# Eight buffers for the index rows of the samples, half of them filled twelve steps early by the other lane

## The reference, cut to what matters

```python
k_idx_all = jnp.concatenate([cache_a_kidx[page_table].reshape(db, past, IDX_D), k_idx], axis=1)
s = jnp.einsum('bqhd,bsd->bqsh', q_idx, k_idx_all)
score = jnp.einsum('bqsh,bqh->bqs', jax.nn.relu(s), w_idx) * (IDX_D ** -0.5 * IDX_H ** -0.5)
top_v, top_i = lax.top_k(score, k_top)
```

```python
a = jax.nn.gelu(jnp.einsum('nhkd,nd->nhk', W['u_tab'][e], xb))
return jnp.einsum('nhk,nhkd->nd', (g * a).astype(xb.dtype), W['v_tab'][e])
```

## Time and profile before

| what | value |
|---|---|
| runs, us | 2521.28, 2516.00, 2503.99; median 2516.0 |
| profiled execution, us | 2509.73 |
| its span, first to last instruction, us | 2508.0 |
| mean granted TensorE clock | 0.816 |
| index stage in the trace | POOL's first fetch at 1395.95 us, SP's store of the scores at 1499.41 us |

### The profile page before, as it was taken

The page is one execution under the profiler, slowest core; times in us unless marked ns, Lnnn a source line. Parts: engine busy times, 40 slices in busy tenths (PEclk is TensorE's granted clock), DMA queues, the critical chain, the costliest instruction groups (busy, mean ns, idle before and its releaser), DMA issues.

```text
span 2508.0 us, 25145 instructions
## 1 busy us (share of the span) xinstructions
PE 1859.6 (74%) x6697; PEld 1011.6 (40%) x6697; DVE 1735.6 (69%) x3914; ACT 700.6 (28%) x2084; POOL 850.7 (34%) x830
## 2 busy tenths in 40 slices
PE   7999889989799978974876686577774362965355
PEld 3458476654333333422322573344441232651021
DVE  3443567441448988589999779987558885786775
ACT  2000156640133443233332222223222121221222
POOL 1000023220023333244555443236226775332442
PEclk9899988999999989987989557788886565557657
DMA  4213150017169999588989889989999999989987
GB/s 132 59 63 104 30 194 1 1 80 323 68 268 382 382 399 376 233 366 342 417 342 420 318 334 388 385 331 400 354 357 381 345 383 418 356 336 425 380 333 313
DMA packets 171529, 722.39 MB, mean 288 GB/s; under 512 B 39706, under 2 KB 83123, under 8 KB 99387
## 3 DMA queue, kind: packets, MB, share of 16 engines
q0 software_dynamic: 84384, 577.16, 57.7%
q1 hardware_dynamic: 85426, 139.95, 15.5%
q10 hardware_dynamic: 1576, 3.66, 0.4%
HBM read 713.16 MB, written 11.61 MB: 289 GB/s over the span
## 4 chain that ended last, share of the span: by engine, by line
PE 20%; DVE 18%; DMA 14%; issue 11%; SPq 5%; POOL 3%; ACT 1%; DVEq 0%; another core or an unknown queue 0%; POOLq 0%; ACTq 0%
DVE heads_t L3762 5%; PE ex_y_ps L3824 4%; DMA ex_pairs<-in_uv_tab,e_idx 3%; DMA heads_t<-in_uv_tab,e_idx 3%; SPq L1345 3%; PE fq_mg_g_ps L2994 2%; SPq L1344 2%; PE sl_at_l_ps L2010 2%; DMA cmp_v<-in_uv_tab,e_idx 1%; DVE branch_rows_t L3767 1%; DMA branch_rows_t<-in_uv_tab,e_idx 1%; DVE heads_t L3767 1%; DVE ex_pairs L3767 1%; PE fq_mg_u_ps L3001 1%; DMA is_ch<-in_cache_a_kidx,chunk_rows 1%
## 5 line engine op out<-in xcount | busy, mean ns | idle before, releaser
L3790 ACT ACTIVATE ex_coef<-ex_dots 128x1 f32<-128x1 f32 x512 | 103.8, 203 | 1040.2 <-DVE ex_dots L3767 960.0
L3733 POOL DMA_INDIRECT ex_pairs<-in_uv_tab,e_idx x147 | 178.2, 1212 | 453.0 <-DVE heads_t L3762 177.2
L3733 POOL DMA_INDIRECT branch_rows_t<-in_uv_tab,e_idx x159 | 197.3, 1241 | 266.9 <-DVE heads_t L3762 179.9
L3733 POOL DMA_INDIRECT heads_t<-in_uv_tab,e_idx x146 | 171.7, 1176 | 252.5 <-DVE heads_t L3762 138.4
L3767 DVE CUSTOM_DVE_ANT_0 ex_pairs<-ex_pairs,heads_t 128x1024 f32<-128x1024 f32 x147 | 179.3, 1221 | 95.0 <-DMA ex_pairs<-in_uv_tab,e_idx 93.9
L3767 DVE CUSTOM_DVE_ANT_0 branch_rows_t<-branch_rows_t,heads_t 128x1024 f32<-128x1024 f32 x159 | 194.0, 1222 | 59.0 <-DMA branch_rows_t<-in_uv_tab,e_idx 54.2
L3767 DVE CUSTOM_DVE_ANT_0 heads_t<-heads_t 128x1024 f32<-128x1024 f32 x146 | 178.1, 1221 | 73.3 <-DMA heads_t<-in_uv_tab,e_idx 70.8
L848 PE MATMUL in_acc<-in_w,xn_t 128*128 128x512 f32 (+7 forms) x560 | 211.5, 534 | 6.1 <-POOLq L196 4.4
L3824 PE MATMUL ex_y_ps<-ex_pairs,heads_t 128*128 128x512 f32 x212 | 118.1, 689 | 75.1 <-ACT heads_t L3797 67.2
L3824 PE MATMUL ex_y_ps<-branch_rows_t,heads_t 128*128 128x512 f32 x224 | 125.3, 693 | 57.4 <-ACT heads_t L3797 50.7
L3792 ACT ACTIVATE ex_coef<-ex_coef,e_gate 128x1 f32<-128x1 f32 x512 | 150.8, 295 | 16.6
(11 more groups left out here) (772 smaller groups left out, 3517.5 us busy)
## 6 DMA issues: line engine op xcount, KB each, us to landing
cs_ch<-in_cache_cmp_kv SPq DMA_DIRECT2D x256, 128.0 KB
fq_wg<-in_w_gate SPq DMA_DIRECT2D x9, 2048.0 KB, 11.9
fq_wb<-in_w_branch SPq DMA_DIRECT2D x9, 1024.0 KB, 16.8
in_w<-in_w_in SPq DMA_DIRECT2D x4, 2048.0 KB, 11.6
fs_blocks<-in_w_branch SPq DMA_DIRECT2D x6, 1024.0 KB, 19.9
heads_t<-in_w_mem_kv SPq DMA_DIRECT2D x4, 1024.0 KB, 5.5
bias_t<-tmp_bias_back SPq DMA_DIRECT2D x4, 1024.0 KB, 9.5
ex_pairs<-in_w_gate SPq DMA_DIRECT2D x2, 2048.0 KB, 25.1
```

The lines of the kernel that those rows point to most:

```text
L3733: pool.indirect_dma_start(out=pair(s), out_offset=None, in_=i["uv_tab"], in_offset=bass.IndirectOffsetOnAxis(ap=idx[:, t, m:m + 1], axis=0 ...
L3790: act.activation(c, dots[:, t, m:m + 1], ACT.Gelu_apprx_tanh).then_inc(gelu_done, 1)
```

## The change

The index rows get eight buffers. Four of them are the halves of the two tiles of `compressed_space()`, four remain in the tile is_ch, which keeps its shape [128, 4, 1024]. Fetches 0 to 3 are issued by a stage of their own in the lane `aside`, which begins 12 steps ahead of the index stage: steps 197 to 209, with yields at 0, 1/4, 1/2 and 3/4 of it, which is ahead of gathers 200, 203, 206 and 209 on POOL. It waits for the last early use of the borrowed tiles. In the index stage POOL issues fetches 4 to 7 at the beginning, and fetch u from 8 on at the share (u - 6.4)/17, after a wait until unit u - 8 is transposed.

```diff
+INDEX_AHEAD = 12
...
-        NU, NBUF = 2 * DB, 4
+        NU, NBUF = 2 * DB, 8
+        view = i["cache_a_kidx"].rearrange("n (c r) w -> (n c) (r w)", r=STRIDE)
+        lane = self.beside
         with ctx:
-            ch = self.sb("is_ch", [P, NBUF, STRIDE * DH], F32, ctx)
+            late = self.sb("is_ch", [P, NBUF // 2, STRIDE * DH], F32, ctx)
+            ch = [x[:, D * n:D * n + D] for x in self.compressed_space() for n in range(2)] + [late[:, n] for n in range(NBUF // 2)]
...
+            def fetch(pool, u):
+                pool.indirect_dma_start(out=ch[u % NBUF], out_offset=None, in_=view,
+                                        in_offset=bass.IndirectOffsetOnAxis(ap=self.row_of[:, u:u + 1], axis=0)).then_inc(ch_in[u % NBUF], 16)
+
+            self.beside, self.aside.next_step = self.aside, lane.next_step - INDEX_AHEAD
+            with self.block(INDEX_AHEAD) as block:
+                @block.gpsimd
+                def _(pool):
+                    mix_done, acc_done = self.mix_sems[2][4:6]
+                    _, dve_upto, pe_upto = v_counts()
+                    pool.wait_ge(mix_done, pe_upto[ROW_MOVES - 1])
+                    pool.wait_ge(acc_done, dve_upto[ROW_MOVES - 1])
+                    for u in range(NBUF // 2):
+                        yield u / (NBUF // 2)
+                        fetch(pool, u)
+
+            self.beside = lane
             with self.block(INDEX) as block:
...
                 @block.gpsimd
                 def _(pool):
-                    view = i["cache_a_kidx"].rearrange("n (c r) w -> (n c) (r w)", r=STRIDE)
-                    for u in range(NU):
+                    for u in range(NBUF // 2, NU):
                         if u >= NBUF:
-                            yield (u - 1) / (NU + 1)
+                            yield (u - NBUF + 1.6) / (NU + 1)
                             pool.wait_ge(turned, 2 * (u - NBUF + 1))
-                        pool.indirect_dma_start(out=ch[:, u % NBUF, :], out_offset=None, in_=view,
-                                                in_offset=bass.IndirectOffsetOnAxis(ap=self.row_of[:, u:u + 1], axis=0)).then_inc(ch_in[u % NBUF], 16)
+                        fetch(pool, u)
...
-                                last = pe.transpose(tr[:, bank, P * k:P * k + P], ch[:, u % NBUF, c0:c0 + P], ident[:])
+                                last = pe.transpose(tr[:, bank, P * k:P * k + P], ch[u % NBUF][:, c0:c0 + P], ident[:])
```

## The result

The changed kernel takes 2500.2 us in the median of 20 runs (2487.0 to 2516.0), the kernel before 2516.8 us in 20 (2500.0 to 2534.7). The ratio is 0.9944 with a 95% interval of 0.9919 to 0.9969, which is 14 us less, between 8 and 20. The one execution that was profiled took longer than that of before (span 2514.2 us against 2508.0), though the median of the runs is lower: two spans can't be compared here, stretches can. They are cut by POOL's gathers, counted by their buffers as ahead of the prediction. Pair 197 was gathered at 1336.81 us before and pair 240 at 1503.39, 166.6 us apart.

The account below looks back on a forecast made before the run. DVE, PE and DMA were all near full in the index stage, with late index-row fetches costing DVE waits. Terms -11.0 + 1.3 + 2.0 = -7.7, rounded to -8, took 2516.0 to 2508 us; range 2496 to 2522.

Parts of the forecast that it names:

- Part 1: Index stage: longer lead of fetches removes DVE's waits for transposes and products, 7.8 + 3.2 = 11.0 us gained.
- Part 2: Ahead of the index stage: four early fetches in a full DMA queue cost 1.3 us, between 0 and 6.4.
- Part 3: First half of the index stage: fetches written early crowd the pairs, new DVE waits of 2 us, between 0 and 4.5.
- The sum: Whole kernel: -11.0 + 1.3 + 2.0 = -7.7 us, giving 2508 us; its own bounds 2505 to 2516.
- The upper price of a fetch: DMA time of one fetch, bounded from above at 1.6 us by the mixed stretch from 1404 to 1490 us.
- (a): Index stage: DMA engines are the bound and the gain turns into waits for pairs; 2513 us, chance 0.22.
- (b): Ahead of and in the index stage: early fetches delay all pairs behind them, so slower; 2521 us, chance 0.08.
- (c): Index and next stage: PE's clock rises above 0.50, added costs vanish, next stage gains some 3 us; 2500 us, chance 0.14.
- (d): Early stage held until the index stage begins, eight fetches in one burst ahead of pair 212; 2513 us, chance 0.03.
- One that was named as wrong: Sign against the forecast: a later stage that grows by what the index stage gives back.
- about 98 us for 103.5: Sign for the forecast: index stage from first index work to the store of the scores, about 98 us for 103.5.

Follow-up runs that it names:

- lead4: The change with fetches from 4 on written 4.1 steps ahead of their transposes; gather 197 to 240 took 158.0 us, profiled once, no ratio.
- early_only: The change with only fetches 0 to 3 early, later ones some 2.5 steps ahead of their transposes as before; ratio 0.9992 to the kernel before.
- ring_only: The change without its early stage: eight buffers, fetches 0 to 7 in one burst at the index stage's start; ratio 0.9981 to the kernel before.
- crowded: The change plus four unused fetches in the first half of the index stage; gather 197 to 240 took 163.2 us, profiled once, no ratio.
- unused_early: The kernel before plus four unused fetches into the borrowed tiles at the change's early places; ratio 0.9988 to the kernel before.

## Why the prediction held, point by point

**Part 1, 11.0 us of waits that go.** Of DVE's 12.7 us of waits for copies and products 1.7 were to be left; 2.7 were, in both profiles, in one single wait at the end. Against the second profile of before (10.5) 7.8 us went. What the step had right is shown by lead4 and early_only: fetches with 2.5 steps of lead were late, and 4.1 steps end it. What it had wrong is that the lead alone would bring this: ring_only brought 3.0 us. It also put fetches 0 to 3 "9 to 12 steps ahead of the stage". By their yields they stand 12, 9, 6 and 3 steps ahead of it, which is 9 to 13 ahead of their transposes; that is still cover enough, and no term rests on it.

**Part 2, 1.3 us for the early fetches.** 1.6 us were measured, alone and in the change. That the first fetch costs DVE its whole time up to dot product 201 and the others nearly nothing came out (0.24, 1.16 and 0.27 us). But the part was entered only as a cost, with the words that no bytes leave the full queue. Four fetches did leave the stage's queue, and crowded prices that at 5.0 us. The sum came out because the change has both halves; the account of which half earns what did not.

**Part 3, 2 us of new waits for pairs, 0 to 4.5.** There were 1.4 and 0.8 us in the stage.

**The sum** of -7.7 us is the stretch's -7.5 (-8.1 and -6.9 by pairs of profiles). The three terms as measured add up to -7.0 in the first pair and -5.3 in the second. Each is within some 1 us of its forecast, but for part 1 against the second profile of before, which is 3.2 off. The runs say -14 and -11. The sum lies at the edge of the first interval (8 to 20 less) and inside the second (4 to 19), so it isn't refuted, but no stretch of the trace shows the rest. The median of 2500.2 lies outside the 2505 to 2516 that the sum's own bounds gave. It is in the stated range because that was drawn wider, for scatter and for the rivals; this much of the hit is luck. The upper price of a fetch, 1.6 us, is worked out from 83.5 us of full work, where 86 us at a share of 0.985 are 84.7; it comes to 1.6 to 1.7 and changes no bound by more than 0.4 us.

**The rivals.** (a) had its mechanism right and its result wrong: the DMA engines leave no slack, as crowded shows, but the four fetches that left the stage were enough to let nearly all of the 11 us come out, and waits for pairs were 1.4 us, not 8. (b) is out by unused_early. (c) named 2500 us, which is what the runs gave, and yet it is out: the clock stays at 0.50 in the stage, and gather 240 to 300 reads 223.9 and 224.0 us for 224.4 and 223.6, so the next stage gained nothing. Its number is a coincidence as far as the traces show. (d) is out: fetch 0 goes out at 1351.40.

**The signs.** One that was named as wrong did show in the first pair of profiles: gather 240 to 344 grew by 11.7 us, more than the stretch gave back. The second profiles took it away, for before grew by 14.3 us there and the change shrank by 10.6. Another sign was not its own sum's: "about 98 us for 103.5" for the stage doesn't follow from -11 + 2, which gives 94.5; 93.6 us were measured between the same two marks.

## What to carry to other kernels

Where a fetch is late by little and the DMA engines are nearly full as well, late transfers and bytes in the stretch can be two limits in a row: test each half alone before one is credited, and price the bytes by adding unused ones. The farthest place for an early transfer is not the cheapest: twelve steps ahead it cost 1.6 us, two steps ahead nothing that shows up to gather 211. In a program whose engines go in steps by a fixed table, check the later stages when one is shortened: one step off cost at least as much as the whole change gave, most of it in two short transfers that an engine waits for.

## What the runs showed that was not expected

One kernel, profiled twice, took 394.9 and 409.2 us from gather 240 to 344, and 35 of its runs in one series lie between 2500.6 and 2532.3 us. The two courses part at gather 304, where it reads 236.3 and 245.2 us behind gather 240 after agreeing to 1 us at gather 300. From gather 240 to 300, by contrast, twelve profiles of twelve executions and ten programs lie within 2.3 us, so a loss of 10 us there is no scatter. Differences of a few us of such a kernel are better read from a stretch of the trace than from its span, once two profiles of one kernel have shown how quiet that stretch is.
